# Seven reorderings of instructions in a two-block transformer kernel on one Trainium2 core

## What is computed

```
layer 0:  half SwiGLU (1024 -> 2816 -> 1024); Mamba-2 mixer; half SwiGLU
layer 1:  half SwiGLU; latent attention (MLA), 16 heads; half SwiGLU
block 2:  y = gm * (mLSTM   @ w_mlstm_out)
            + gd * (diffatt @ w_diff_out)
            + gr * (retention @ w_ret_out)      # gm, gd, gr: sigmoid gates of 1024
          x = x + rms(y @ w_out);  x = x + rms(SwiGLU(x))
```

## Time and profile before

| | |
|---|---|
| median of 3 runs | 1745.78 us (1745.45 to 1746.18) |
| the profiled execution's own time | 1745.42 us |
| its span, first to last instruction | 1743.6 us |
| PE busy | 1719.9 us, 99% of the span |
| ACT, DVE busy | 877.4 us (50%), 1214.1 us (70%) |
| mean granted clock of TensorE | 0.997 of full speed |
| read from HBM | 296.21 MB, 170 GB/s |

### The profile page before, as it was taken

One profiled execution on the slowest core, in us unless ns is written; L12 is line 12 of the kernel. 1 busy time (PEld: TensorE's weight loads), 2 busy tenths in 40 slices (PEclk: granted clock), 3 DMA queues, 4 the chain that ended last, 5 costly groups with the idle time before them and its releaser, 6 DMA issues.

```text
span 1743.6 us, 24848 instructions
## 1 busy us (share of the span) xinstructions
PE 1719.9 (99%) x9532; PEld 1486.9 (85%) x9532; DVE 1214.1 (70%) x1394; ACT 877.4 (50%) x1085; POOL 99.6 (6%) x141
## 2 busy tenths in 40 slices
PE   8999999999999999999999999999999999999998
PEld 7888899888888888889888888988887888878887
DVE  7766799675776686767767676876557675567666
ACT  5444575765444454445864444765337634444443
POOL 0000031130000000002500000000000100000000
PEclk9999999999999999999999999999999999999999
DMA  8555465324655556553336655554554554446552
GB/s 271 189 181 191 131 210 168 117 97 145 217 188 183 183 193 192 187 178 112 124 120 218 192 188 167 170 193 143 183 183 144 166 186 134 166 141 233 184 192 81
DMA packets 214386, 298.27 MB, mean 171 GB/s; under 512 B 12518, under 2 KB 170283, under 8 KB 214315
## 3 DMA queue, kind: packets, MB, share of 16 engines
q1 hardware_dynamic: 214250, 297.27, 52.4%
q10 hardware_dynamic: 64, 0.02, 0.0%
HBM read 296.21 MB, written 1.05 MB: 170 GB/s over the span
## 4 chain that ended last, share of the span: by engine, by line
PE 90%; DVE 4%; issue 3%; ACT 2%; DMA 1%; POOL 1%; SPq 0%; POOLq 0%; DVEq 0%; ACTq 0%
PE PS L458 27%; PE PS L464 14%; PE PS L340 12%; PE PS L341 11%; PE PS L414 7%; PE PS L359 4%; PE PS L449 2%; PE PS L450 1%; PE PS L451 1%; PE PS L334 1%; PE PS L336 1%; PE PS L335 1%; DVE wlo L323 1%; PE PS L747 1%; DVE conv_acc L1156 1%
## 5 line engine op out<-in xcount | busy, mean ns | idle before, releaser
L318 ACT ACTIVATE whi<-raw 128x2048 fp32r<-128x2048 f32 (+3 forms) x286 | 535.2, 1872 | 415.0 <-PE PS L464 314.2
L323 DVE TENSOR_TENSOR wlo<-raw,whi 128x2048 fp32r<-128x2048 f32 (+3 forms) x286 | 639.4, 2239 | 138.6 <-ACT whi L318 138.1
L458 PE MATMUL PS<-XT,whi 128*128 128x512 f32 x2016 | 506.6, 394 | 3.1 <-ACT whi L803 2.1
L458 PEld LDWEIGHTS PS<-XT,whi 128*128 128x128 f32 x2016 | 368.2, 190 | 72.8 <-issue 4.0
L464 PEld LDWEIGHTS PS<-XT,wlo 128*128 128x128 f32 x2016 | 273.9, 190 | 19.2 <-DVE wlo L323 0.4
L464 PE MATMUL PS<-XT,wlo 128*128 128x256 f32 x2016 | 280.8, 282 | 0.0
L341 PE MATMUL PS<-whi,aT 128*128 128x512 f32 x400 | 156.3, 391 | 0.0
L340 PE MATMUL PS<-whi,aT 128*128 128x512 f32 x400 | 156.2, 390 | 0.0
L340 PE MATMUL PS<-whi,XT 128*128 128x512 f32 (+2 forms) x320 | 125.6, 394 | 0.1
L341 PE MATMUL PS<-whi,XT 128*128 128x512 f32 (+2 forms) x320 | 122.2, 383 | 0.0
L642 ACT ACTIVATE aT<-ff_a 128x512 fp32r<-128x512 f32 x50 | 31.6, 631 | 172.1 <-PE PS L414 162.9
(11 more groups left out here) (432 smaller groups left out, 2252.1 us busy)
## 6 DMA issues: line engine op xcount, KB each, us to landing
raw<-in_w_in SPq DMA_DIRECT2D x112, 512.0 KB, 4.4
raw<-in_ffn_w_up SPq DMA_DIRECT2D x88, 512.0 KB, 4.4
raw<-in_ffn_w_down SPq DMA_DIRECT2D x88, 512.0 KB, 4.1
raw<-in_ffn_w_gate SPq DMA_DIRECT2D x87, 512.0 KB, 4.5
raw<-in_ssm_w_in SPq DMA_DIRECT2D x48, 512.0 KB, 4.5
raw<-in_w_ffn_in SPq DMA_DIRECT2D x44, 512.0 KB, 4.2
raw<-in_w_ffn_out SPq DMA_DIRECT2D x22, 512.0 KB, 4.1
raw<-in_ssm_w_out SPq DMA_DIRECT2D x16, 512.0 KB, 4.1
```

The source lines that it names most:

```text
L318: act.activation(whi[s][:, 0:size], raw[s][:, 0:size], ACT.Copy).then_inc(hi_done, 1)
L323: dve.tensor_tensor(wlo[s][:, 0:size], raw[s][:, 0:size], whi[s][:, 0:size].bitcast(FP32), ALU.subtract).then_inc(lo_done, 1)
L458: return pe.matmul(o, whi[n % SLOTS][:, sl], XT[:, k, :, :].rearrange("p a n -> p (a n)"), start=(k == 0), stop=False)
```

## The change

1. `mul_features` waits first for the high half of its block alone, does all products with whi of its first half of the features, and only then waits for wlo.
2. At the end of the feature stage one of four z steps stands ahead of the turning of b = 6 and three ahead of that of b = 7; all four stood ahead of b = 6.
3. `scores(g)` does sums and diagonal of `psG[:, 0]`, then of `SEG2`, then the two products `C B^T`, then sums and diagonal of `psG[:, 1]`; for g = 0 it waits for `nat` 7 at its start and for `nat` 8 ahead of the last pair. Before, the three sums came first, then the three diagonals, then `C B^T`, after a wait for `nat` 8.
4. `Z_STEPS`: the slot behind outputs(3) has three steps (it had two), that behind outputs(6) one (it had two).
5. `high(1)` and `low(1)` move from the loop of the projection into the iteration of the last group: on ACT ahead of the squares, on DVE ahead of the split of the next block.
6. In the latent attention, `c_hi(3)` and `c_hi(4)` move ahead of the high split of block kv1, and `left_hi(1)` ahead of the exponentials of head 12.
7. The turning of y's block 0 moves into the last product of `w_ret_out`, ahead of its last three products.

```diff
 def mul_out(... by_half=None, turn_within=None):
             for c in range(2):
                 for k in range(2):
                     for t in range(NT):
+                        if (c, k, t) == (1, 1, 1):
+                            turn_within()
                         m = mul_out_part(pe, n, lefts, t, k, first, last, bank, (c,))
...
 def mul_features(pe, n, bank, it=0):
-            wait_block(pe, n, it)
+            wait_high(pe, n, it)
             for c in range(2):
+                o = bank[:, c * SEQ:(c + 1) * SEQ]
                 for k in range(KD):
                     pe.matmul(o, whi[s][:, sl], XTh[:, k, :], start=(k == 0), stop=False)
                     pe.matmul(o, whi[s][:, sl], XTl[:, k, :], start=False, stop=False)
-                    m = pe.matmul(o, wlo[s][:, sl], XTh[:, k, :], start=False, stop=(k == KD - 1))
+                if c == 0:
+                    wait_block(pe, n, it)
+                for k in range(KD):
+                    m = pe.matmul(o, wlo[s][...], XTh[:, k, :], start=False, stop=(k == KD - 1))
...
-        Z_STEPS = [0, 4, 8, 11, 13, 16, 18, 20, 22, 24]
+        Z_STEPS = [0, 4, 8, 11, 13, 16, 19, 21, 23, 24]
...
-                if i == NXB:
-                    z_steps(0)
+                if i >= NXB:
+                    z_range(0 if i == NXB else 1, 1 if i == NXB else Z_STEPS[1])
...
 scores(g), g == 0:
-                    pe.wait_ge(A["nat"], 8)
+                    pe.wait_ge(A["nat"], 7)
...
-                for o, sums in ((psG[:, 0, :], ...), (psG[:, 1, :], ...), (SEG2, ...)):
-                    pe.matmul(o..., heads, sums, start=True, stop=False)
-                for o in (psG[:, 0, :]..., psG[:, 1, :]..., SEG2...):
-                    pe.matmul(o, ident_r[:, :], masked[:, 0:P]..., start=False, stop=True)
+                sums_of(psG[:, 0, :], ...)      # one product with heads, one with ident_r
+                sums_of(SEG2, ...)
                 pe.matmul(psT[:, 0:SEQ], BC[:, g, 0:P], BC[:, SSM_G + g, :], start=True, stop=True)
-                pe.matmul(psT[:, SEQ:TRI], ...).then_inc(A["b"], 1)
+                pe.matmul(psT[:, SEQ:TRI], ...)
+                if g == 0:
+                    pe.wait_ge(A["nat"], 8)
+                sums_of(psG[:, 1, :], ...).then_inc(A["b"], 1)
...
 ssm_act, loop over g:
                 hi_upto(act, at, nz + Z_AHEAD[g + 1])
+                if g == SSM_G - 1:
+                    high(1)
...
-                high(g)
+                if g > 1:
+                    high(g)
...
 ssm_dve, loop over g:
-                if g == 6:
-                    low(0)
+                if g >= 6:
+                    low(g - 6)
                 lo_upto(dve, at, nz + Z_AHEAD[g + 1])
...
-                low(g)
+                if g > 1:
+                    low(g)
...
 mla_act:
-            hi_upto(act, at, N["kv1"])
             for c in range(3, 5):
                 c_hi(c)
+            hi_upto(act, at, N["kv1"])
...
+                if h == 12:
+                    left_hi(1)
                 if h < MH:
                     act.wait_ge(M["nm"], h + 1)
...
                 if h == 12:
-                    left_hi(1)
                     hi_upto(act, at, N["mla_out"] + 2)
...
 b2_pe:
-            project_pe(pe, B, N["ret_out"], ..., by_half=B["half"])
-            turn_y(range(2))
+            project_pe(pe, B, N["ret_out"], ..., by_half=B["half"],
+                       turn_within=lambda: turn_y(range(1)))
+            turn_y(range(1, 2))
```

More of the change, by code:

```diff
@@ L390, in mul_out_held, with mul_out @@
             m.then_inc(block_used, 1)
-        def mul_out(pe, n, it, lefts, first, last, bank=lambda t, c: psD[:, 2 * t + c, :], by_half=None):
+        def mul_out(pe, n, it, lefts, first, last, bank=lambda t, c: psD[:, 2 * t + c, :], by_half=None,
+                    turn_within=None):
             if by_half:
@@ L443, in mul_features @@
             s = n % SLOTS
-            wait_block(pe, n, it)
+            wait_high(pe, n, it)
             for c in range(2):
+                o = bank[:, c * SEQ:(c + 1) * SEQ]
                 for k in range(KD):
                     sl = slice(k * 2 * P + c * P, k * 2 * P + (c + 1) * P)
-                    o = bank[:, c * SEQ:(c + 1) * SEQ]
                     pe.matmul(o, whi[s][:, sl], XTh[:, k, :], start=(k == 0), stop=False)
                     pe.matmul(o, whi[s][:, sl], XTl[:, k, :], start=False, stop=False)
-                    m = pe.matmul(o, wlo[s][:, sl], XTh[:, k, :], start=False, stop=(k == KD - 1))
+                if c == 0:
+                    wait_block(pe, n, it)
+                for k in range(KD):
+                    m = pe.matmul(o, wlo[s][:, k * 2 * P + c * P:k * 2 * P + (c + 1) * P], XTh[:, k, :], start=False,
+                                  stop=(k == KD - 1))
             m.then_inc(block_used, 1)
@@ L924, in left_dve, with project_pe @@
                                   Xh[:, 2 * b:2 * b + 2, :].bitcast(FP32), ALU.subtract).then_inc(S["ll"], 1)
-        def project_pe(pe, S, n, Xh, Xl, base, cells, hold, turn_rest=None, by_tile=None, by_half=None):
+        def project_pe(pe, S, n, Xh, Xl, base, cells, hold, turn_rest=None, by_tile=None, by_half=None,
+                       turn_within=None):
             for b in range(4):
@@ L940, in project_pe @@
                 else:
-                    mul_out(pe, n + b, 0, left, False, b == 3, by_half=by_half if b == 3 else None)
+                    mul_out(pe, n + b, 0, left, False, b == 3, by_half=by_half if b == 3 else None,
+                            turn_within=turn_within)
         posi = sb("posi", [P, NT], I32)
@@ L1015, in z_steps, with z_range @@
             def z_steps(slot):
-                step = Z_STEPS[slot]
-                while step < Z_STEPS[slot + 1]:
+                z_range(Z_STEPS[slot], Z_STEPS[slot + 1])
+            def z_range(step, end):
+                while step < end:
                     k, s0 = 2 + step // 4, step % 4
-                    s1 = min(4, s0 + Z_STEPS[slot + 1] - step)
+                    s1 = min(4, s0 + end - step)
                     q, h = k // 2, k % 2
@@ L1071, in scores, with sums_of @@
                 heads = of_group[:, g:g + 1].to_broadcast([2 * SSM_HEADS, P])
-                for o, sums in ((psG[:, 0, :], by_rank[:, 0:2, :]), (psG[:, 1, :], by_rank[:, 2:4, :]),
-                                (SEG2, by_rank[:, :, P:SEQ])):
+                def sums_of(o, sums, diagonal):
                     pe.matmul(o.rearrange("p (r n) -> p r n", n=sums.shape[-1]), heads, sums, start=True, stop=False)
[L1075 to L1079, removed]
-                pe.matmul(psT[:, 0:SEQ], BC[:, g, 0:P], BC[:, SSM_G + g, :], start=True, stop=True)
-                pe.matmul(psT[:, SEQ:TRI], BC[:, g, P:SEQ], BC[:, SSM_G + g, P:SEQ], start=True, stop=True)\
-                  .then_inc(A["b"], 1)
+                    return pe.matmul(diagonal, ident_r[:, :],
+                                     masked[:, 0:P].unsqueeze(1).to_broadcast([P, diagonal.shape[1], P]),
+                                     start=False, stop=True)
+                sums_of(psG[:, 0, :], by_rank[:, 0:2, :], psG[:, 0, :].rearrange("p (r n) -> p r n", n=SEQ)[:, :, 0:P])
+                sums_of(SEG2, by_rank[:, :, P:SEQ], SEG2.rearrange("p (r n) -> p r n", n=P))
+                pe.matmul(psT[:, 0:SEQ], BC[:, g, 0:P], BC[:, SSM_G + g, :], start=True, stop=True)
+                pe.matmul(psT[:, SEQ:TRI], BC[:, g, P:SEQ], BC[:, SSM_G + g, P:SEQ], start=True, stop=True)
+                if g == 0:
+                    pe.wait_ge(A["nat"], 8)
+                sums_of(psG[:, 1, :], by_rank[:, 2:4, :], psG[:, 1, :].rearrange("p (r n) -> p r n", n=SEQ)[:, :, 0:P])\
+                    .then_inc(A["b"], 1)
             def outputs(g):
@@ L2192, in b2_pe @@
             gate_chunks(pe, N["gr"], 7, lambda: left_pe(pe, B, xn, lambda b: (B["hs"], 2 + b // 2 + 1)))
-            project_pe(pe, B, N["ret_out"], HTh, HTl, 8, BY_TILE, (B["gev"], 10), by_half=B["half"])
             def turn_y(of):
                 left_pe(pe, B, Y, lambda b: (B["yv"], 3 + b), of)
-            turn_y(range(2))
+            project_pe(pe, B, N["ret_out"], HTh, HTl, 8, BY_TILE, (B["gev"], 10), by_half=B["half"],
+                       turn_within=lambda: turn_y(range(1)))
+            turn_y(range(1, 2))
             project_pe(pe, B, N["y_out"], HTh, HTl, 12, BY_HALF, (B["y1"], 1), lambda: turn_y(range(2, 4)), by_tile=BY_TILE)
```

## The result

The changed kernel takes 1749.01 us (median of 19 runs, 1747.98 to 1749.96), the kernel before 1745.61 us (median of 19 runs on the same chips). The ratio is 1.0018, with a 95% interval of 1.0012 to 1.0024: 2.1 to 4.2 us more. The forecast was +2.2 us and 1748.0. So the change made the kernel slightly slower, by about as much as one measurement can just tell.

A forecast was written before the change was run, and what follows sets the result against it. TensorE, busy 99% of the span, was taken as the bound. A cost of 6.1 us less savings of 3.9 gave +2.2, so 1748.0 us from 1745.78; the forecast's own range was 1746.7 to 1749.3, the whole range 1741.9 to 1749.7.

The forecast's parts named there:

- Changes of rows: In `scores(g)`, six changes between 64-row and 128-row operands instead of two, 0.195 us each over eight groups: +6.1 us.
- The start of the scan: At scores(0), the wait for `nat` 8 is covered but a stall appears at the turning of b = 6: net -0.2 us.
- `gTl`: At the projection behind the scan, moving `high(1)` and `low(1)` earlier removes PE's wait for `gTl`: -1.1 us.
- `wlo`: In `mul_features`, the one block where PE waits for wlo needs it 16 products later: -0.7 us.
- `XT`: In the latent attention, `left_hi(1)` ahead of the exponentials uses idle ACT time and removes the wait for `XT`: -0.7 us.
- `HTl`: At `w_ret_out`, turning y's block 0 three products earlier shrinks a wait of 0.9 us to about 0.4: -0.7 us.
- Part 4: `Z_STEPS`: a third step removes the 0.8 us wait for `mix`, with a new 0.3 to 0.4 stall at outputs(7): net -0.4.
- Part 6, `cTl`: In the latent attention, `c_hi` ahead of the split of kv1 wins only 0.14 of the 0.5 us wait: -0.1 us.
- free-changes rival: In `scores(g)`, changes of rows cost nothing, so only the savings of 3.9 us remain: 1741.9 us; chance 0.16.
- The rival in which the wait for `gTl` only moves: At the projection, the wait moves to `low(2)` and the next product, so part 5 gives nothing: +3.3, 1749.1 us; chance 0.10.

The follow-up runs named there:

- e3: The changed kernel with its sums taken over 128 rows, the lower 64 rows of `of_group` being zeros, order as changed; 1740.14 us.
- e4: The changed kernel with the first two sums of `scores(g)` together, then their diagonals: four changes of rows a group instead of six; 1745.71 us.
- e5: The changed kernel with `Z_STEPS` as before, two steps behind outputs(3) and two behind outputs(6); 1748.08 us.
- e1: The kernel before with only the new order of products inside `scores(g)`, its waits staying at the start; 1751.09 us.
- e11: The changed kernel with 128-row sums, old `Z_STEPS`, `C B^T` last for g > 0, and z steps two and two around turning b = 6; 1740.38 us.
- e10: The changed kernel with 128-row sums, `C B^T` last for g > 0, and z steps dealt anew, three behind scores(0) instead of four; 1747.75 us.

## Why the prediction was nearly right

**Changes of rows, +6.1.** Right in mechanism and size: 6.2 (eight times 0.78 in the traces), and e3 and e4 show that it is rows, counted by changes. **The start of the scan, -0.2.** As forecast: the first sum starts at 313.60 instead of 313.40, while the feature stage ahead of it ran 0.41 later, so this stretch is 0.2 shorter. The wait has moved to the turning, where it is 0.6 truly. **`gTl`, -1.1; `wlo`, -0.7; `XT`, -0.7; `HTl`, -0.7.** Measured, start against start, 1.1, 0.7, 0.7 and 0.7 of loss gone. For y, three products before the next wait moved everything by just their length.

**Part 4, -0.4.** This is the step that failed. Its sign was wrong: it cost 1.0, as e5 shows, and the 0.8 for `mix` was won by the dearer order, as e1 shows. Two errors stand in it. The slack of 1.17 us ahead of outputs(7) was measured to `mix` only, while outputs(g) also waits for `y_read`, raised by the sum into `dxs` that DVE does right behind `mix`; its true slack was 0.58 less the 0.15 that a start takes, 0.4, and 1.37 - 0.4 is the 1.0 seen. And the wait at scores(5) was taken as fixed, though the longer scores ahead of it, costed in the same text, could eat it, and did in e1.

**Part 6, `cTl`, -0.1.** Nothing. ACT's timeline in the changed kernel:

```profile
826.17 0.82 ACT L1683 ACTIVATE cn<-PS 128x768 f32<-128x768 f32 x1
827.84 0.84 ACT L1669 ACTIVATE cTh<-PS,cols 128x256 fp32r<-128x256 f32 x2 [0.86 <-PE PS L1509]
828.57 1.06 ACT L318 ACTIVATE whi<-raw 128x1024 fp32r<-128x1024 f32 x1
```

The split of kv1 now stands behind, and ACT idles 0.86 us in its place until PE has turned: with the stage's shift of 5.55 us, `c_hi` begins at the same moment as in the earlier trace rows. The split had filled idle time; the prediction had the turned latents ready at 822.15, 0.14 too early.

The sum of the terms as measured is 6.2 - 0.2 - 0.8 + 1.0 - 1.1 - 0.7 - 0.7 - 0.7 = +3.0, within the interval of 2.1 to 4.2. The spans differ by 2.9, in which two shares of the single execution nearly cancel: the changed kernel lost 0.4 us within its first 16, where products have nothing to do with the change (eight transposes take 1.91 us from 11.71 on, 1.03 in before), and around the last norm it met a higher clock (0.79 over 1549 to 1557 us, against 0.62 over the same stretch of before, 1545.5 to 1553.5), which gave 0.6 back.

The free-changes rival needed a distance of 0.23 us from sum to diagonal, and it was 0.42. The rival in which the wait for `gTl` only moves named 1749.1 us, and 1749.01 was measured; by the number alone it would have won over the forecast. The trace rejects it, since no wait for `gTl` is left. Of the 0.8 us by which the measured terms exceed the forecast, part 4 is 0.6 (-0.8 + 1.0 against -0.4). The rest of the distance to +3.4, the difference of the medians, lies within the interval and is not explained.

The forecast's own range also has a slip: costs of 5.4 to 6.4 less savings of 3.4 to 4.4 give +1.0 to +3.0, 1746.8 to 1748.8 us, and not up to 1749.3. The measured median lies in the range as written and just outside the one that its terms give.

## What to carry to other kernels

Group products by the number of rows of their operands, or pad those of 64 rows with zeros to 128. What is shown is 64 beside 128; 96 beside 128 cost nothing. On a TensorE that never waits, an order chosen to cover a wait can cost more in changes than the wait. Before time is taken out of a slot, list every semaphore on which the work behind it waits, not only the one that ended last, and every buffer that what is moved writes. Price the parts in the order in which they act: a slower part may already have covered the wait that the next one is to remove.

## What the runs showed that was not expected

More rows were cheaper: a product with 64 rows of zeros added cost 0.235 us to its successor where the narrow one cost 0.42.

The granted clock fell in single places behind a wait of 0.8 to 0.9 us shown, to means between the levels 1.2 and 2.4 GHz: 0.57 over 316 to 320 us in e1, 0.64 over 384 to 388 in e4 and 0.54 over 380 to 382 in e11. Each time it cost some 1.5 us. The kernel before stood in front of the same wait as e1, at 313.40, and kept 1.00 behind it, and e1's profiled execution took 1752.7 us where its median is 1751.1. So such a fall comes in some executions of a kernel and not in others, though e10, whose PE waits most, has a lower mean clock in five of eleven. Terms of a few tenths can only be read from stretches whose clock is compared first.
